# A hybrid decoder step on one Trainium2 core: attention scores on half of the array's rows, the queries stored once, and both maps of a head issued side by side while a score row fits one PSUM bank

## What the kernel computes

```
xn = rms_norm(h)
[qa|ka|va|qb|kb|vb|ga|gb] = xn @ w_in                       # 1024 -> 5120
# branch A, 4 heads, two maps each (q1|q2 and k1|k2, 64 columns each), values 128 wide
p = softmax(q1 k1^T / 8 + bias) - lam * softmax(q2 k2^T / 8 + bias);  o_a = p @ v
# branch B, 8 heads of 64: stick-breaking attention
z = q k^T / 8;  A = sigmoid(z) * suffix product of sigmoid(-z);  o_b = A @ v
h = h + (sigmoid(ga) * proj(o_a) + sigmoid(gb) * proj(o_b)) @ w_out
# PEER: each token picks 8 x 16 = 128 of 16384 experts by two lists of 128 sub-keys
act = gelu(xn . peer_u[idx]);  h = h + sum(gate * act * peer_v[idx])
y = rms_norm(h)
```

## Time and profile before

| | |
|---|---|
| median of 3 runs | 3580.61 us (3579.76 to 3584.66) |
| time of the profiled execution | 3589.16 us |
| its span, first to last instruction | 3587.3 us |
| TensorE busy | 2813.8 us, 78% |
| VectorE busy | 2717.2 us, 76% |
| ScalarE busy | 955.1 us, 27% |
| GpSimd busy | 2280.3 us, 64% |
| DMA | 377 GB/s over the span |

### The profile page before, as it was taken

How to read it: one execution, slowest core, us unless ns; L and a number is a source line. 1 busy time by engine, 2 the same in 40 slices (tenths; PEclk the granted TensorE clock), 3 DMA queues, 4 the chain that set the end, 5 groups by cost and what they waited for, 6 DMA issues and landing times.

```text
span 3587.3 us, 29094 instructions
## 1 busy us (share of the span) xinstructions
PE 2813.8 (78%) x7732; PEld 1268.2 (35%) x7732; DVE 2717.2 (76%) x5688; ACT 955.1 (27%) x1911; POOL 2280.3 (64%) x2225
## 2 busy tenths in 40 slices
PE   8999978987896677777777777777787786677755
PEld 6644433333342333233334332433253242222211
DVE  5314887998788967897879687977897676778775
ACT  5322311122122322242224222422242133312210
POOL 1001566677667766776777677776777565566776
PEclk9999999999998879988998899999989998779878
DMA  7543999999999999999999999999999999999998
GB/s 262 185 151 136 341 419 418 410 397 407 419 410 394 401 415 414 414 380 407 415 411 374 408 419 398 371 407 419 410 365 398 410 385 373 372 401 409 412 402 353
DMA packets 398868, 1353.36 MB, mean 377 GB/s; under 512 B 44806, under 2 KB 48902, under 8 KB 397554
## 3 DMA queue, kind: packets, MB, share of 16 engines
q0 software_dynamic: 316080, 1149.15, 80.6%
q1 hardware_dynamic: 62162, 163.81, 12.3%
q10 hardware_dynamic: 20464, 38.54, 2.9%
HBM read 1323.53 MB, written 27.80 MB: 377 GB/s over the span
## 4 chain that ended last, share of the span: by engine, by line
DMA 15%; POOL 14%; PE 9%; issue 7%; DVE 6%; ACT 1%; DVEq 0%; ACTq 0%; POOLq 0%
POOL t_ring L1302 14%; DMA t_ring<-in_peer_v,t_idx 10%; DMA t_ring<-in_peer_u,t_idx 4%; PE ps L1556 4%; PE ps L1391 3%; DVE t_ring L2108 2%; DVE t_acc L2141 1%; DMA t_big<-in_w_out 1%; DMA t_big<-in_peer_w_query 1%; PE ps L1361 1%; PE ps L1330 1%; ACT t_pTr L1583 0%; PE ps L1507 0%; DVE t_big L1888 0%; PE ps L1520 0%
## 5 line engine op out<-in xcount | busy, mean ns | idle before, releaser
L1556 PE MATMUL ps<-t_ring,t_diag 128*128 128x512 f32 (+1 forms) x2346 | 1280.4, 668 | 454.4 <-DMA t_ring<-in_peer_v,t_idx 430.8
L1302 POOL DMA_INDIRECT t_ring<-in_peer_u,t_idx x1088 | 1103.7, 1014 | 748.8 <-issue 257.4
L2108 DVE CUSTOM_DVE_ANT_0 t_ring<-t_ring,ps 128x1024 f32<-128x1024 f32 x1088 | 1319.5, 1215 | 324.9 <-DMA t_ring<-in_peer_u,t_idx 319.0
L1302 POOL DMA_INDIRECT t_ring<-in_peer_v,t_idx x1088 | 1153.0, 1060 | 415.0 <-issue 263.1
L1556 PEld LDWEIGHTS ps<-t_ring,t_diag 128*128 128x128 f32 (+1 forms) x2346 | 422.6, 200 | 1164.6 <-DMA t_ring<-in_peer_v,t_idx 824.5
L2141 DVE SCALAR_TENSOR_TENSOR t_acc<-t_ring,t_wgt,t_acc 128x1024 f32<-128x1024 f32 x403 | 519.2, 1288 | 101.0 <-DMA t_ring<-in_peer_v,t_idx 93.5
L1538 PE MATMUL ps<-val,keyT 128*128 128x512 f32 x800 | 380.7, 614 | 34.1 <-DMA val<-in_w_in 26.5
L1391 PE MATMUL ps<-t_big,t_pTr 128*128 128x512 f32 x696 | 343.3, 638 | 64.6 <-DMA t_big<-in_w_out 20.3
L1748 ACT ACTIVATE t_diag<-ident,t_wgt 128x128 f32<-128x128 f32 x649 | 249.0, 398 | 539.2 <-PE ps L1556 513.5
L1583 ACT COPY t_pTr<-ps 128x512 f32<-128x512 f32 (+3 forms) x216 | 110.6, 512 | 548.6 <-PE ps L1330 547.6
L1391 PEld LDWEIGHTS ps<-t_big,t_pTr 128*128 128x128 f32 x696 | 135.1, 202 | 261.6 <-issue 146.7
(11 more groups left out here) (239 smaller groups left out, 2291.7 us busy)
## 6 DMA issues: line engine op xcount, KB each, us to landing
t_big<-in_peer_w_query SPq DMA_DIRECT2D x72, 512.0 KB, 7.9
t_big<-in_w_out SPq DMA_DIRECT2D x65, 512.0 KB, 7.9
wraw<-in_w_in SPq DMA_DIRECT2D x40, 512.0 KB, 5.4
val<-in_w_in ACTq DMA_DIRECT2D x40, 512.0 KB, 9.2
t_ring<-in_peer_u,t_idx POOLq DMA_INDIRECT x1088, 7.2
t_ring<-in_peer_v,t_idx POOLq DMA_INDIRECT x1088, 7.2
t_big<-in_w_proj_sb SPq DMA_DIRECT2D x19, 512.0 KB, 10.8
proj_d<-val ACTq DMA_DIRECT2D x36, 256.0 KB, 5.8
```

The source lines that it names most:

```text
L1302: pool.indirect_dma_start(row(kind, e, s), None, table, bass.IndirectOffsetOnAxis(ap=idx[:, e % 2, s:s + 1], axis=0)).then_inc(s_ring[g % ...
L1556: m = nc.tensor.matmul(ps[0:n, c, :], diag[:, pe_place[e, s] % NDG, 0:n], row("v", e, s)[:, c * CH:(c + 1) * CH], start=s == pe_rows_of(e, ...
L2108: nc.vector.tensor_tensor_reduce(out=row("u", e, s), in0=row("u", e, s), in1=x_row, scale=1.0, scalar=0.0, op0=ALU.mult, op1=ALU.add, accu ...
```

## The change

1. `take_queries` copies each group of queries once, scaled by 1/8, into `qT_all` of eight blocks of 128 columns. `half_scale` and its four memsets go.
2. `pe_scores` contracts over 64 rows: map 0 uses partitions 0 to 63 of queries and keys, map 1 partitions 64 to 127.
3. In turns 0 to 3 the scores of map 1 are issued right behind those of map 0, two beats earlier than before for pairs 0 to 3 and three beats for pairs 4 to 7, with all the waits that they had. In turns 4 to 7 the order stays.
4. `aside` grows from 8 to 16 columns, in the place that `half_scale` leaves. `ring` and all other buffers keep their addresses.

```diff
-        half_scale = keep("half_scale", [P, 2])
-
-        aside = keep("aside", [P, 8])
+
+        aside = keep("aside", [P, 16])
...
-                        for m in range(2):
-                            nc.vector.memset(half_scale[64 * m:64 * m + 64, m:m + 1], 0.125)
-                            nc.vector.memset(half_scale[64 * m:64 * m + 64, 1 - m:2 - m], 0.0)
...
-            qz = slots(9, 11).rearrange("p (u m r) -> p u m r", m=2, r=P)
+            qT_all = big[:, 9, :].rearrange("p (u r) -> p u r", r=P)
...
                 for c in range(0, kw, CH):
                     wide = min(CH, kw - c)
-                    m = nc.tensor.matmul(scores_of(t, hf)[:, c:c + wide], qz[:, u, hf, :], keyT[:, u, c:c + wide],
+                    rows = slice(64 * hf, 64 * hf + 64)
+                    m = nc.tensor.matmul(scores_of(t, hf)[:, c:c + wide], qT_all[rows, u, :], keyT[rows, u, c:c + wide],
                                          start=True, stop=True)
...
                 elif kind == "scores":
-                    pe_scores(pe, t, *which)
+                    u, hf = which
+                    if width(t) > CH:
+                        pe_scores(pe, t, u, hf)
+                    elif hf == 0:
+                        pe_scores(pe, t, u, 0)
+                        pe_scores(pe, t, u, 1)
...
-                    nc.scalar.activation(qz[:, 4 * g:4 * g + 4, 0, :], src, ACT.Copy, scale=half_scale[:, 0:1])
-                    act_T.raised_by(nc.scalar.activation(qz[:, 4 * g:4 * g + 4, 1, :], src, ACT.Copy, scale=half_scale[:, 1:2]))
+                    act_T.raised_by(nc.scalar.activation(qT_all[:, 4 * g:4 * g + 4, :], src, ACT.Copy, scale=0.125))
```

## The result

| | before | after |
|---|---|---|
| median of 16 runs each | 3587.78 us | 3598.95 us |
| lowest and highest | 3577.29 to 3597.35 us | 3586.88 to 3609.48 us |
| profiled execution, its span | 3587.3 us | 3597.9 us |

The ratio is 1.0027, with a 95% interval of 1.0017 to 1.0036: 9.7 us slower, between 6.1 and 12.9. The kernel before is itself 7.2 us above the 3580.61 of the three runs that I predicted from; put on that scale, the ratio gives 3590.3 us. So the size is inside my range of 3570 to 3598 (the raw median is 0.95 us above it), but the change is slower by more than 0.2% (7.2 us), the side to which I gave 0.29, and not "within 0.2%"; the lower end of the interval, 6.1 us, is still within. One kernel's runs scatter over 20 us, so a single profile says little of a total; what follows goes by stages first.

A forecast was written before the change was run, and what follows sets the result against it. Bound by TensorE's list in turn 0, then mainly DMA, with tight TensorE or VectorE stretches late. +1.6 (turn 0) - 1.2 (copies) - 0.1 (turn 1 scores) + 2.5 (turns 4 to 7) = +2.8 us: 3583.5 us, range 3570 to 3598.

The forecast's parts named there:

- What bounds the kernel: Turn 0: mostly TensorE's own list; DMA carries turns 2 onward; in turn 7 TensorE and VectorE are each tight in single stretches.
- The price of a visit: Each visit of TensorE to half height costs 0.42 us, whatever the columns: 0.23 entering and leaving, 0.19 on the neighbour.
- the visit is free: Rival: changing height costs TensorE nothing, so turns 4 to 7 lose nothing; 3576 us, still within 0.2%; chance 0.05.
- the halves don't overlap: Rival: the two half-height matmuls don't run side by side; turns 0 and 1 lose 6.7 us; 3588.6 us; chance 0.02.
- Turn 0 and the copies: Turn 0: side by side costs TensorE 1.6 us, and dropping ScalarE's second query copy gains 0.58 us there.
- The earlier maps and the earlier wait: Turn 1's 4.46 us VectorE stall moves to pair 5; turn 2's 3.2 us TensorE wait is covered; both booked at nothing.
- "takes" rival: Turns 0 and 1: VectorE's waits for second maps were on the path; 14 to 18 us faster, about 3565; chance 0.16.
- Turns 4 to 7: 64 lone half-height score pieces cost 26.9 us of TensorE; twelve on the chain bound what lands at 5.0; booked +2.5.
- slower: the late visits land: Rival: half-height visits in turns 4 to 7 land, all giving 3608 us, half 3594; decides from 17 of 64; chance 0.27.
- main case: Whole kernel: no change within 0.2% (7.2 us) of 3580.6, about 3583.5 us, own range 3574 to 3591; chance 0.50.
- no chance of its own: Half height pulling the granted clock from 2.4 to 1.2 GHz got no separate chance, though one 20 us stretch would outweigh all terms.
- a clear fall of turn 7's clock: Sign of being wrong: turn 7's granted clock falling clearly below its 0.93.

The follow-up runs named there:

- e12: Kernel before with half height and one query copy in all eight turns, nothing side by side: 3604.62 us, ratio 1.0047, 16.9 us over before.
- e2: Kernel before with half height and one query copy in turns 4 to 7 only, nothing side by side: 3591.62 us, ratio 1.0019.
- e3: Kernel before plus, in turns 4 to 7, one 8-column half-height matmul ahead of each map's full-height scores: 3593.65 us, ratio 1.0018.
- e4: Kernel before plus, in turns 4 to 7, one 8-column full-height matmul ahead of each map's scores: 3591.14 us, ratio 1.0010.
- e5: Kernel before plus 512-column matmuls at the end of TensorE's list, full or half height, with or without pauses; groups of 2 with pauses: 42.3 us full, 66.9 us half.
- e9: Kernel before plus end-of-list groups of two 512-column matmuls (full or half height) and 16 full-height 128-column ones; longest pause: 148.60 us full, 160.50 us half.
- e10: Kernel before with half height and one query copy in turns 6 and 7 only: 3595.09 us, ratio 1.0019.
- e11: Kernel before with half height and one query copy in turns 4 and 5 only: 3588.18 us, ratio 1.0002.
- e1: Changed kernel with turns 4 to 7 back at full height and two query copies: 3588.83 us, ratio 1.0010.
- e6: Changed kernel plus, in turns 4 to 7, a 256-column matmul on the other half of the rows beside each map's first 512 score columns: 3599.0 us, ratio 1.0041.
- e7: Changed kernel plus, in turns 4 to 7, a 256-column matmul on the map's own rows behind its first 512 score columns: 3617.91 us, ratio 1.0081.
- e8: Kernel before, full height everywhere, with only the change's order of score maps in turns 0 to 3: 3588.4 us, ratio 1.0000.

## Why the prediction was right or wrong

**What bounds the kernel** was read rightly: turn 0 by TensorE (shown by e12), turns 1 to 5 by transfers (their lengths moved by at most 1.0 us in the changed kernel), single stretches of turns 6 and 7 by TensorE.

**The price of a visit** was 0.42 us, measured 0.39 between neighbours (0.21 behind a pause), and the halves overlap. The rivals "the visit is free" and "the halves don't overlap" are out.

**Turn 0 and the copies**: +1.6 - 0.6 = +1.0 us at the first indices; they came at 339.1 us instead of 340.2. But the eight kernels here with turn 0 of before (before, e2, e3, e4, e5, e9, e10, e11) have them between 338.8 and 341.6 us, and the four with turn 0 of the change (after, e1, e6, e7) between 339.1 and 340.6, so a term of this size is not resolved. That TensorE's time lands in turn 0 is shown, by e12.

**The earlier maps and the earlier wait** were booked at nothing, and the order alone measured 0 us [-3.9, 3.6] (e8). Its first indices came at 336.7 us, 2.1 us before the earliest of all others, so in turn 0 the order may give some 2 us that I had at nothing; in one trace this is not shown. The "takes" rival, with its faster kernel, is out: the stall of 4.46 us was no path.

**Turns 4 to 7 is the step that failed.** I wrote that "the twelve pieces on the chain bound it: 12 x 0.42 = 5.0 us", and took half of it. Turns 4 and 5 did stay as they were, but 6 and 7 did not:

| turns 6 and 7, us | | mean |
|---|---|---|
| full height there (before, e1, e5, e8, e9, e11) | 760.1, 760.4, 762.2, 763.5, 761.4, 757.9 | 760.9 |
| half height there (after, e2, e10, e12) | 770.9, 773.8, 765.4, 765.6 | 768.9 |

The term is 8.0 us by these means, where I had booked 2.5 and had 5.0 as its upper end. All four kernels with half height lie above that 2.5 (by 4.5 to 12.9 us over the mean of the six); that the term is above 5.0 rests on the mean, since two of the four lie at 4.5 and 4.7. The chain is not a bound: it names what came last at each step of one execution, and it moves with the kernel. In the changed kernel it passes through nine score pieces in turn 7 in place of six, three of them later than any of before, and through two in turn 4 and four in turn 5, where it had none and where the lengths stayed. From the chain that ended last, turn 7 after the change:

```profile
2603.19 2.00 PE ps L1358 x4
...
2626.52 1.91 PE ps L1358 x4
...
2632.94 1.93 PE ps L1358 x4
```

Why more lands is argued and not shown: in a stretch in which TensorE is full, a piece pushes all that is behind it, whether the chain passes through it or not. How much of an added time lands there has no fixed share in these runs: 12.4 of 13.2 us between e6 and e7, but 2.7 of 16.6 us in e3 and nothing of 10.9 us between the changed kernel and e6. 32 visits of 0.39 us are at most 12.5 us, so visits alone could carry the 8.0.

The rival that came nearest was "slower: the late visits land": the loss of 9.7 us is past the 7.1 from which it decides. But it asked for 17 visits or more out of 64 and knew nothing of the clock, so it is borne out in its place (turns 6 and 7) and its sign, not in its whole mechanism. That my range of 3570 to 3598 held is partly luck: its main case ended at 3591, and the rest of the upper side was there for this rival.

**The clock had "no chance of its own"**, because no row of before showed half height pulling it down. Before had half height only in the key scores, 288 records of 128 columns in groups of 16 that use both halves in turn, 20.9 us of TensorE's time in all; that is no evidence either way. The fall is real: in the first 150 us of turns 6 and 7 there are 51.2, 51.2, 64.8 and 54.6 us at 1.2 GHz with full height there (before, e1, e8, e11; e5 and e9 have 61.4 and 58.0), and 71.6, 81.9, 75.1 and 75.0 us with half height (after, e2, e10, e12). The 20 us more are 10 us of work at full speed if TensorE was busy throughout. I had named a clear fall of turn 7's clock as a sign of being wrong; it fell from 0.93 to 0.91, which is little beside the 0.92 of e8 at full height. The fall shows in the sums over several turns.

**What stays open** is how the 8.0 us divide. Visits (up to 12.5 us of TensorE's time) and clock (up to 10) overlap with its idle time in ways that no run took apart. The run with visits and no half-height streaming (e3) lost 2.7 us in turns 6 and 7 for 32 x 0.52 = 16.6 us, which speaks for the clock; its control (e4) lost 6.0 for 7.0, which speaks against reading either so closely. Six profiles of kernels with the same code in turns 6 and 7 differ there by up to 5.6 us.

No version here beats the kernel before. Side by side in turns 0 to 3 with full height after them (e1) is 3.6 us above it [-0.7, 7.9].

## What to carry to other kernels

Half height can pay only where the other half really works beside it: alone, it streams no faster, costs 0.39 us a visit, and can cost clock. Bound a cost in a late stage by all its instructions there, not by those that the chain of one execution happens to name: 12 pieces gave 5.0 us, 32 give 12.5, and 8.0 were measured. Before a form of matmul that a kernel hardly has is spread over it, measure its clock with the pauses of the real stage; streamed without a pause it looks harmless.

## What the runs showed of the hardware

- With the same columns and pauses, groups of two or four matmuls on 64 rows ran at a granted clock of 0.54 and 0.52, on 128 rows at 1.00 (e5); without a pause, 150 on 64 rows stayed at 1.00 for 129 us (e9).
- The fall costs at the return too: the 24 full-height matmuls behind such a stretch had 0.93 and took 22.4 us in place of 20.9.
- ScalarE's one query copy takes 0.60 us, as this row at the start of turn 0 shows, where each of the two with a scale per partition took 0.68 to 0.69:

```profile
155.92 0.60 ACT L1610 ACTIVATE t_big<-ps 128x512 f32<-128x512 f32 x1 [1.20 <-PE ps L1326]
```
